# Last projection of the second mixer: the third chunk's first half of the contraction, its cast and its low part moved between the two merges

## The reference

```python
    merged = jax.nn.sigmoid(ga) * (ya @ w_br_fox) + jax.nn.sigmoid(gb) * (yb @ w_br_dsa)
    return merged @ w_out
...
    x = x + mod[:, 1, 2][:, None, :] * y
    h = modulate(x, norm_g[l, 2], mod[:, 2, 0], mod[:, 2, 1])
    x = x + 0.5 * mod[:, 2, 2][:, None, :] * swiglu(h, ffn2_w1[l], ffn2_w3[l], ffn2_w2[l])
```

## Time and profile before

| | |
|---|---|
| median of 3 runs | 1039.13 us (1038.64 to 1039.34) |
| the profiled execution: its own time | 1039.31 us |
| its span in the trace | 1037.4 us |
| mean granted TensorE clock | 0.992 of full |
| busy: PE, DVE, ACT | 97%, 77%, 48% of the span |

### The profile page before, as it was taken

One profiled execution on the slowest core, in us unless ns is written; L12 is line 12 of the kernel. 1 busy time (PEld: TensorE's weight loads), 2 busy tenths in 40 slices (PEclk: granted clock), 3 DMA queues, 4 the chain that ended last, 5 costly groups with the idle time before them and its releaser, 6 DMA issues.

```text
span 1037.4 us, 18809 instructions
## 1 busy us (share of the span) xinstructions
PE 1005.7 (97%) x7584; PEld 952.2 (92%) x7587; DVE 795.4 (77%) x1196; ACT 498.3 (48%) x599; POOL 2.1 (0%) x5
## 2 busy tenths in 40 slices
PE   5999999999999999999999999999999999999998
PEld 5999868899999999899999998988988999999997
DVE  5897973689998888799888887888954858644545
ACT  4698263543443445544343445555456464343441
POOL 0000000000000000000000000000000000000000
PEclk8999999999999999999999999999999999999999
DMA  7753321467877767379988965653332557765541
GB/s 220 249 167 122 123 81 42 164 201 244 283 242 244 243 204 244 122 265 345 310 312 294 318 193 132 194 162 94 112 122 82 165 168 238 246 200 169 195 162 41
DMA packets 163150, 199.93 MB, mean 193 GB/s; under 512 B 13216, under 2 KB 138138, under 8 KB 163098
## 3 DMA queue, kind: packets, MB, share of 16 engines
q1 hardware_dynamic: 163098, 199.20, 59.2%
HBM read 198.13 MB, written 1.05 MB: 192 GB/s over the span
## 4 chain that ended last, share of the span: by engine, by line
PE 77%; DVE 14%; issue 4%; ACT 4%; DMA 1%; SPq 0%; DVEq 0%; ACTq 0%
PE psX L1716 15%; PE psX L1717 14%; PE psX L1718 14%; PE psA L1716 4%; PE psA L1717 4%; PE psA L1718 4%; DVE wlo L938 3%; PE psX L1748 2%; PE psX L1749 2%; PE psA L1723 2%; PE psA L1724 2%; PE psA L1725 2%; ACT whi L493 2%; PE psX L1758 2%; PE psX L1808 1%
## 5 line engine op out<-in xcount | busy, mean ns | idle before, releaser
L938 DVE TENSOR_TENSOR wlo<-raw,whi 128x2048 fp32r<-128x2048 f32 x151 | 346.3, 2295 | 110.4 <-ACT whi L493 109.4
L493 ACT CAST whi<-raw 128x2048 fp32r<-128x2048 f32 x150 | 285.3, 1906 | 267.1 <-PE psX L1718 164.7
L1716 PE MATMUL psX<-hh,whi 128*128 128x256 f32 x1400 | 402.2, 287 | 2.6 <-DVE wlo L938 1.8
L1717 PE MATMUL psX<-hl,whi 128*128 128x256 f32 x1400 | 396.8, 283 | 0.0
L1718 PE MATMUL psX<-hh,wlo 128*128 128x256 f32 x1400 | 396.7, 283 | 0.0
L1716 PEld LDWEIGHTS psX<-hh,whi 128*128 128x128 f32 x1400 | 268.8, 192 | 8.0 <-issue 2.6
L1717 PEld LDWEIGHTS psX<-hl,whi 128*128 128x128 f32 x1400 | 268.8, 192 | 1.9 <-issue 1.4
L1718 PEld LDWEIGHTS psX<-hh,wlo 128*128 128x128 f32 x1400 | 268.8, 192 | 0.0
L1288 DVE SCALAR_TENSOR_TENSOR adacc<-scr,small,adacc 128x256 f32<-128x256 f32 (+1 forms) x175 | 105.4, 602 | 5.8
L1716 PE MATMUL psA<-oh,whi 128*128 128x256 f32 x384 | 109.6, 286 | 0.0
L1717 PE MATMUL psA<-ol,whi 128*128 128x256 f32 x384 | 108.8, 283 | 0.0
(11 more groups left out here) (333 smaller groups left out, 1303.0 us busy)
## 6 DMA issues: line engine op xcount, KB each, us to landing
raw<-in_ffn_w SPq DMA_DIRECT2D x66, 1024.0 KB, 5.4
scr<-in_ada_w SPq DMA_DIRECT2D x36, 1024.0 KB, 7.4
raw<-in_w_in SPq DMA_DIRECT2D x33, 1024.0 KB, 5.4
raw<-in_w_ffn_gate SPq DMA_DIRECT2D x11, 1024.0 KB, 5.4
raw<-in_w_ffn_up SPq DMA_DIRECT2D x11, 1024.0 KB, 5.5
raw<-in_w_ffn_down SPq DMA_DIRECT2D x11, 1024.0 KB, 5.0
raw<-in_w_out SPq DMA_DIRECT2D x8, 1024.0 KB, 5.1
raw<-in_w_ple_gate SPq DMA_DIRECT2D x4, 1024.0 KB, 5.3
```

What stands on the lines that cost most here:

```text
L493: a_.copy(whi[b % 3][:, :], raw[b % 3][:, :]).then_inc(sem("hi_ready"), 1)
L938: v_.tensor_tensor(wlo[b % 3][:, :], raw[b % 3][:, :], whi[b % 3][:, :].bitcast(F32), ALU.subtract).then_inc(sem("lo_ready"), 1)
L1716: pe.matmul(dst, wh, xh, start=start, stop=False, skip_group_check=True)
L1717: pe.matmul(dst, wh, xl, start=False, stop=False, skip_group_check=True)
```

## The change

On ACT, the cast of chunk 116 (`hi(OUT2 + 2)`) moves from behind the fourth merge step's cast to between the third and the fourth. On DVE, the low part of chunk 116 (`lo(OUT2 + 2)`) moves from behind the fourth merge step to between the third and the fourth. On PE, chunk 116 is cut like the other two: its first half of the contraction comes ahead of the second half of chunk 114, its second half behind that of chunk 115. Nothing is added or removed.

```diff
@@ ACT
                     k = 4 * c + 2 * t
                     a_.copy(hh[:, k:k + 2, :], mg).then_inc(sem("mg_hi"), 1)
+                    if c and t == 0:
+                        hi(OUT2 + 2)
             for j in range(4):
-                hi(OUT2 + j + 2)
+                if j:
+                    hi(OUT2 + j + 2)
@@ DVE
                     v_.tensor_tensor(hl[:, k:k + 2, :], mg, hh[:, k:k + 2, :].bitcast(F32),
                                      ALU.subtract).then_inc(sem("mg_lo"), 1)
+                    if c and t == 0:
+                        lo(OUT2 + 2)
             for j in range(4):
-                lo(OUT2 + j + 2)
+                if j:
+                    lo(OUT2 + j + 2)
@@ PE
             for pairs in ((0, 1), (2, 3)):
-                for j in range(2):
+                for j in range(3):
                     merged(j, pairs)
-            gemm(OUT2 + 2, psA[:, 2, :], hh, hl)
```

## The result

The changed kernel takes 1041.3 us (median of 20 runs, 1036.6 to 1043.12) where the kernel before takes 1038.39 (20 runs, 1033.43 to 1039.81). The ratio is 1.0028, with a 95% interval of 1.0015 to 1.0041: between the medians the change costs 2.9 us (1.6 to 4.3 by the interval), and the forecast was 3.03 on top of the time before. The times of both kernels come in groups: of the 20 runs of before nine took 1033.4 to 1035.6 us and eleven 1038.4 to 1039.8, of those of the change six 1036.6 to 1037.1 and fourteen 1038.9 to 1043.1. Both medians lie in the upper group.

What follows compares the result with a forecast made beforehand. PE, busy for 97% of the span, was taken as the bound, so its stalls count in full. The wait's +1.54 us and the clock's +1.49 made +3.03 on 1039.13, so 1042.2 us, range 1040.3 to 1043.5.

Steps and rivals of the forecast that it cites:

- The start of the cast: On ACT, chunk 116's cast starts 0.53 us after the start of merge step 3's cast, at 817.65.
- The low part: On DVE, chunk 116's low part starts 1.93 us after its cast and runs from 819.58 to 821.87.
- PE's loss: At chunk 116's first half, PE starts 3.06 us late and loses 3.16 where it lost 1.62.
- The wait's net cost: On PE, the wait for chunk 116's low part costs +1.54 us over the old stall.
- The covers: Behind the stall, PE reaches merge step 4 with 1.2 us to spare and chunk 117 with 1.3.
- The clock: Behind PE's 2.90 us gap, the clock falls from 2.4 to 1.2 GHz, costing 1.49 us.
- B: Rival at PE's gap: the stall comes as reckoned but the clock stays up, +1.54, 1040.7 us; 24%.
- C: Rival behind PE's gap: the clock stays down longer, price 2.54, in all +4.1, 1043.2 us; 10%.
- D: Rival on PE: chunk 116's first half bridges the wait for merge step 4, -1.62, 1037.5 us; 4%.
- The total: Whole kernel: 1.54 for the wait plus 1.49 for the lower clock, +3.03 us, giving 1042.2 us.

Runs made afterwards that it cites:

- e2: The changed kernel with the cast of chunk 116 alone moved up on ACT, right behind that of chunk 115; stretch 42.60 us, ratio to before 1.0011.
- e4: The changed kernel with 12 matmuls of zeros filling PE's gap ahead of the first half of chunk 116; stretch 43.78 us, ratio 1.0015.
- e3: The changed kernel with PE's order put back to that of before, keeping the moves on ACT and DVE; stretch 47.15 us, ratio 1.004.
- e5: The kernel before with the change's order on PE alone, without the moves on ACT and DVE; stretch 48.76 us, ratio 1.0054.
- e1: The changed kernel with cast and low part of chunk 116 moved ahead of merge step 3; stretch 41.57 us, ratio to before 0.9995.
- e6: The kernel before with the cast of chunk 114 moved on ACT to between merge steps 1 and 2; stretch 41.07 us, ratio 0.9986.
- e9: A repeat profile of the kernel of e2, nothing else changed; stretch 42.58 us, whole time 1033.87 us.
- e7: The changed kernel with casts of chunks 114 and 116 early and PE's order cut in seven pieces; stretch 40.39 us, ratio to before 0.9985.
- e10: Another repeat profile of the kernel of e2, nothing else changed; stretch 42.59 us, whole time 1039.1 us.

## Why the prediction was right

*The start of the cast.* Reckoned 0.53 us behind the cast of merge step 3; it is 816.65 - 816.13 = 0.52. e2 shows that nothing but its place in ACT's list held it: there it starts 11.8 us into the stretch and not 16.4.

*The low part.* Reckoned to follow the cast's start by 1.93 and to hold the next instruction back by 2.21: 1.94 and 2.21.

*PE's loss.* 3.06 late, reckoned and measured (820.94 - 817.88). The wait's net cost was put at 1.54, and e4, which has the wait without the lower clock, shows 1.51.

*The covers.* Merge step 4 is done at 824.18 (823.49 + 0.69) and PE doesn't wait for it. Nor does it for chunk 117, whose cast starts at 828.56; 1.0 added for the later start of before's stretch, this is 829.55, where 828.04 was reckoned, and the difference is the 1.5 us of the slow matmuls, which the reckoning of the covers left out. Neither cover gave way in the two executions of the change: until the next layer the wait for chunk 116 is PE's only one. The margins are best read in e4, at full clock. PE comes to merge step 4 at 823.61 and it was done at 822.45; PE comes to chunk 117 at 830.81 and its low part was done at 829.53. That leaves 1.2 and 1.3, as reckoned.

*The clock.* That it would fall was argued from two other stalls, and the price, 1.49, from one of them. It fell in both profiled executions of the change; 45.32 - 43.78 gives 1.54. The step was right in kind and size. The argument was weaker than it looked: the 2.16 us that lost the clock came from one execution, and the same wait loses it in eight of the twelve profiled executions and keeps it in four (last section). What holds the conclusion up is the longer waits: each wait of 2.7 us or more between two matmuls in these traces, 14 in all, was followed by the lower clock. Executions do differ, then, at a wait near 2.2 us; at the 2.9 of the change the two profiled ones did not. One detail was off: I took the fall to come a microsecond after PE resumes, as at 631.04, and it came with the first matmuls. It did not change the price.

*Rivals.* B, the wait with the clock up, is what e4 shows and was not what happened. C, a price of 2.54, was argued from a longer idle time; e3, idle for 4.8, pays 47.15 - 42.27 - 3.4 = 1.5, and e5, idle for 6.2, pays 48.76 - 42.27 - 4.84 = 1.65 by the same reckoning, so even there it was not reached. D was decided as stated: the low part was done 3.0 us behind the point at which PE asked for it. The working also said that with the cast done in advance a low part between merge steps 3 and 4 would still cost PE 1.98 in place of 1.62; e2 shows 42.60 - 42.27 = 0.33 for that, as against 0.36.

*The total.* +3.03 forecast, +2.9 between the medians and +3.05 in the stretch. The difference was reckoned step by step, and the steps came out. The level is another matter. It was 0.9 too high, 0.74 of that because the median of before over 20 runs is 1038.39 and over the three known ones was 1039.13; the range took it in. There was luck in this: the three known runs were all from the upper group of times, nine of the 20 were not, and with two or three more in the lower group the median of before would have been some 3 to 4 us lower. The range allowed for 0.35 us of scatter, where the runs of one kernel lie up to 6.5 apart.

## What to carry to other kernels

A filler that is to bridge a wait must be ready before the wait begins, with all that it needs: count its own chain (load, cast, low part) against the time at which the engine will ask, and not only whether its buffers are free. And an instruction put into a queue ahead of the work that is being waited for puts that work off by its whole length, 2.2 us in e1, and by its own wait besides, 3.4 in the change. Here two casts stood in ACT's list behind a wait that they did not need. Taking that of chunk 114 out gained 1.2 us on the kernel before (e6), and taking that of chunk 116 out gained 2.7 on the change (e2), where the order on PE gained 1.8 given the moves (e3) and lost 6.5 without them (e5).

## What the hardware showed that was not expected

With matmuls of zeros in the gap the clock stayed up (e4), as it did where PE had real work; this was profiled once, and the whole times agree with it.

How long a wait must be for the clock to fall is not one number. In the stretch, PE idle for 1.35 and for 1.7 us (three times) kept it; 2.9 (twice), 4.8 and 6.2 lost it. Between them lies a wait that all kernels here share, the one of 2.16 to 2.17 us for `hh` near 629, and it goes both ways: the clock fell behind it in eight of the twelve profiled executions, and stayed at 1.00 in four (e2, e9, e4 and e6). At the kernel's start, waits of 2.46 (e4) and 2.50 (e7) kept it and ten of 2.7 to 4.2 lost it. Nor does the longest wait decide alone: near 152 us the clock falls in ten of twelve, with no wait over 1.2 us there.

The same kernel's time varies by 5 to 6 us from one execution to the next, and the clock at these places is where it comes from. Two executions of the kernel of e2, e10 and e9, have stretches of 42.59 and 42.58 us, but take 1039.1 and 1033.87 us, and are apart by 5.1 when the stretch begins, at 800.65 and 795.53. Their windows of 8 us, and PE at the end of the wait near 629, in e10

```profile
152.00:160.00 8.00, 7.95 (x28) 5.97 (x28) 4.85 (x9) 4.28 (x11) 0.00 (x0) 0.57 0.35 100
628.00:636.00 8.00, 6.73 (x44) 6.76 (x45) 7.90 (x17) 5.16 (x10) 0.00 (x0) 0.79 0.68 171
629.27 0.36 PE L1753 MATMUL psX<-hh,whi 128*128 128x256 f32 x1 [2.17 <-ACT hh L520]
```

and in e9, where the same wait ends 3.6 us earlier

```profile
152.00:160.00 8.00, 7.98 (x49) 6.31 (x49) 5.36 (x11) 4.43 (x14) 0.00 (x0) 1.00 0.43 128
624.00:632.00 8.00, 6.36 (x53) 6.39 (x54) 7.59 (x18) 5.52 (x10) 0.00 (x0) 1.00 0.74 178
625.64 0.36 PE L1753 MATMUL psX<-hh,whi 128*128 128x256 f32 x1 [2.16 <-ACT hh L520]
```

show that in one of them PE ran below full clock around 155 and 632 us and in the other it did not. The 5.1 us divide as 0.5 that they are apart ahead of the first place, 3.1 that come in at it and 1.5 at the second. The mean granted clock of whole runs fits: of the 35 runs of before beside e1, the nine up to 1034.01 us have 0.998, and the 21 from 1038.2 have 0.992 or 0.993. That is also why a gain of 1.9 us that is plain in one stretch is hardly seen in a dozen whole times. What decides which way an execution goes was not tested.
